# One masked square a head in the even linear attention, and outputs five steps behind scores in the softmax attentions

## The reference

```python
def step(s, blk):
    qc, kc, vc, gc = blk
    G = jnp.cumsum(gc, axis=2)
    decay = jnp.exp(jnp.where(tri, G[:, :, :, None, :] - G[:, :, None, :, :], -jnp.inf))
    scores = jnp.einsum('bhik,bhjk,bhijk->bhij', qc, kc, decay)
    o = jnp.einsum('bhij,bhjv->bhiv', scores, vc) + jnp.einsum('bhik,bhkv->bhiv', qc * jnp.exp(G), s)
    G_last = G[:, :, -1:, :]
    s = s * jnp.exp(G_last)[:, :, 0, :, None] + jnp.einsum('bhjk,bhjv->bhkv', kc * jnp.exp(G_last - G), vc)
    return s, o
```

## Time and profile before

| What | us |
|---|---|
| median of three runs | 3082.21 |
| the profiled execution, its own time | 3080.94 |
| its span in the profile | 3079.1 |
| TensorE busy | 2976.5 |
| VectorE busy | 732.1 |
| ScalarE busy | 399.4 |
| GpSimd busy | 252.1 |
| even layer's softmax attention | about 217 to 270 |
| GLA | 270 to 378 |
| attentions of the second stack | 1559 to 1595 and 2009 to 2050 |

### The profile page before, as it was taken

One profiled execution on the slowest core, in us unless ns is written; L12 is line 12 of the kernel. 1 busy time (PEld: TensorE's weight loads), 2 busy tenths in 40 slices (PEclk: granted clock), 3 DMA queues, 4 the chain that ended last, 5 costly groups with the idle time before them and its releaser, 6 DMA issues.

```text
span 3079.1 us, 41222 instructions
## 1 busy us (share of the span) xinstructions
PE 2976.5 (97%) x17952; PEld 1702.2 (55%) x17952; DVE 732.1 (24%) x1737; ACT 399.4 (13%) x981; POOL 252.1 (8%) x339
## 2 busy tenths in 40 slices
PE   7999899999999999999999999999999999999998
PEld 3546654444459998667657777454444444444434
DVE  1327722000046665400141001242000000000002
ACT  1114220000022222100031000131000000000001
POOL 2113310000012221200000000000000000000030
PEclk9999999999999999999999999999999999999999
DMA  9860022122122222354335332319999999999993
GB/s 361 320 256 3 15 82 82 60 84 82 57 72 59 76 76 84 117 191 157 122 111 205 143 143 103 127 55 392 361 402 385 385 402 384 384 403 385 384 404 122
DMA packets 214210, 618.59 MB, mean 201 GB/s; under 512 B 6840, under 2 KB 54168, under 8 KB 207504
## 3 DMA queue, kind: packets, MB, share of 16 engines
q1 hardware_dynamic: 206128, 594.30, 50.9%
q0 software_dynamic: 7296, 20.54, 2.0%
q10 hardware_dynamic: 608, 1.12, 0.1%
HBM read 608.67 MB, written 7.26 MB: 200 GB/s over the span
## 4 chain that ended last, share of the span: by engine, by line
PE 91%; DVE 3%; DMA 2%; issue 2%; ACT 1%; PEld 0%; PEldq 0%; POOLq 0%; POOL 0%; DVEq 0%; SPq 0%; ACTq 0%
PE ps_main L677 15%; PE ps_main L719 7%; PE ps_moe_down L3329 6%; PE ps_moe_up L3279 6%; PE ps_moe_gate L3279 6%; PE ps_second L677 6%; PE ps_main L2120 6%; PE ps_lin L1516 4%; PE ps_moe_down L3337 3%; PE ps_moe_gate L3284 3%; PE ps_moe_up L3284 3%; PE ps_second L719 3%; PE ps_main L2143 2%; PE ps_main L564 1%; PE ps_mod L1445 1%
## 5 line engine op out<-in xcount | busy, mean ns | idle before, releaser
L677 PE MATMUL ps_main<-hT,ring_buf 128*128 128x256 f32 (+2 forms) x1408 | 447.9, 479 | 2.4 <-issue 1.6
L677 PEld LDWEIGHTS ps_main<-hT,ring_buf 128*128 128x128 f32 x1408 | 263.7, 190 | 187.0 <-issue 169.2
L719 PE MATMUL ps_main<-ring_buf,ffn_hiddenT 128*128 128x512 f32 x528 | 228.9, 593 | 1.8 <-issue 1.8
L2120 PE MATMUL ps_main<-ring_buf,hT 128*128 128x256 f32 (+1 forms) x992 | 196.1, 352 | 0.3 <-issue 0.3
L677 PE MATMUL ps_second<-hT,ring_buf 128*128 128x256 f32 (+1 forms) x896 | 192.3, 376 | 2.3 <-DMA ring_buf<-in_w_ffn_up_dram 1.0
L3502 DVE TENSOR_TENSOR moe_hidden_buf<-moe_silu_buf,ps_moe_up 128x768 f32<-128x768 f32 (+1 forms) x32 | 27.3, 854 | 664.7 <-PE ps_moe_up L3284 664.7
L677 PEld LDWEIGHTS ps_second<-hT,ring_buf 128*128 128x128 f32 x896 | 167.1, 190 | 28.4 <-issue 5.3
L2120 PEld LDWEIGHTS ps_main<-ring_buf,hT 128*128 128x128 f32 x992 | 166.4, 191 | 17.8 <-issue 0.6
L719 PEld LDWEIGHTS ps_main<-ring_buf,ffn_hiddenT 128*128 128x128 f32 x528 | 99.5, 190 | 127.7 <-issue 127.6
L1516 PE MATMUL ps_lin<-ring_buf,hT 128*128 128x448 f32 (+1 forms) x384 | 133.1, 500 | 1.0 <-ACT hT L1576 1.0
L3279 PE MATMUL ps_moe_up<-ring_buf,moe_xg_buf 128*64 128x512 f32 (+1 forms) x672 | 131.8, 545 | 0.0
(11 more groups left out here) (547 smaller groups left out, 3524.3 us busy)
## 6 DMA issues: line engine op xcount, KB each, us to landing
ring_buf<-in_w_exp_down_dram SPq DMA_DIRECT2D x17, 4096.0 KB, 18.5
ring_buf<-in_w_exp_up_dram SPq DMA_DIRECT2D x16, 4096.0 KB, 18.7
ring_buf<-in_w_exp_gate_dram SPq DMA_DIRECT2D x15, 4096.0 KB, 19.8
mod_pieces<-in_mod_w_dram SPq DMA_DIRECT2D x40, 1024.0 KB, 6.5
moe_third<-in_w_exp_gate_dram SPq DMA_DIRECT2D x9, 4096.0 KB, 19.6
moe_third<-in_w_exp_up_dram SPq DMA_DIRECT2D x8, 4096.0 KB, 19.1
moe_third<-in_w_exp_down_dram SPq DMA_DIRECT2D x7, 4096.0 KB, 18.5
ring_buf<-in_odd_w_in_dram SPq DMA_DIRECT2D x40, 512.0 KB, 6.2
```

The lines of the kernel that those rows point to most:

```text
L677: mm = nc.tensor.matmul(ps[:, lo:wide], view[:, k, i * P:(i + 1) * P], hT[:, k, first_col + lo:first_col + wide], start=k == 0, stop=k == ...
L719: mm = nc.tensor.matmul(ps_y[i % 2][:, h, :], hidT[:, b, i * P:(i + 1) * P], view[:, b, h * 512:(h + 1) * 512], start=first, stop=end)
L2120: mm = nc.tensor.matmul(ps[:, 0:width], hT[:, k, t * P:(t + 1) * P], view[:, k, 0:width], start=k == 0, stop=k == KD - 1)
```

## The change

**In GLA** the two coarsest levels are handled apart. Their scores are made for the blocks alone that the mask would leave, one of 64 x 64 and two of 32 x 32 for each head (`coarse_blocks`), and ScalarE copies these into the square (`take_coarse`). VectorE then lays the other six levels over the same square, one predicated copy each, so that one square a head stays, cleared once at the start; the output has one product a head for it. The scores' banks are split in two: levels 0 to 3, and 4 to 6 with the own keys. TensorE may fill the first once two levels of the unit before have been merged. Sums of the six fine levels use half of the rows (a fine block never crosses the middle of the tile), with 384 columns. The end keys go from VectorE to GpSimd, behind the keys; the total is made by ScalarE. TensorE's list becomes scores(u), output(u-1), sums(u+3).

**In `attend`** there are three probability buffers in place of two. In step i TensorE runs scores(i), turned(i-3), output(i-5); VectorE takes the turned copy ahead of the division. The buffer of turned probabilities keeps two halves.

```diff
@@ gla_pairs @@
-        PLACES, ROUNDS = 2, NL // 2
+        ROUNDS, COARSE = NL - 2, 2
+        HALF, QUARTER = P // 2, P // 4
...
+            def coarse_blocks(d):
+                late, early = (0, 1) if d == 0 else (1, 0)
+                return [(0, late * HALF, early * HALF, HALF)] + \
+                    [(1, x * HALF + late * QUARTER, x * HALF + early * QUARTER, QUARTER) for x in range(2)]
...
                 def sums(u):
                     pe.wait_ge(S["rec_decays"].handle, S["rec_decays"].at(u))
-                    for h in range(2):
-                        nc.tensor.matmul(ps_sums[:, h * 4:h * 4 + 4, :], gs(u), T.sums[:, units[u][1], h * 4:h * 4 + 4, :],
+                    table = T.sums[:, units[u][1], :, :]
+                    for c in range(2):
+                        nc.tensor.matmul(ps_sums[:, c, 0:2, :], gs(u), table[:, 0:2, c * HALF:(c + 1) * HALF],
+                                         start=True, stop=True)
+                    for c in range(2):
+                        own = slice(c * HALF, (c + 1) * HALF)
+                        nc.tensor.matmul(ps_sums[:, c, 2:NL, :], gs(u)[own, :], table[own, 2:NL, own],
                                          start=True, stop=True)
...
-                    pe.wait_ge(S["rec_masked"].handle, S["rec_masked"].at(u))
-                    for l in range(NL - 1):
+                    pe.wait_ge(C["coarse_taken"].handle, C["coarse_taken"].at(u))
+                    pe.wait_ge(S["rec_masked"].handle, S["rec_masked"].at(max(ROUNDS * (u - 1) + 2, 0)))
+                    for l, k0, q0, size in coarse_blocks(d):
                         for e in range(2):
-                            nc.tensor.matmul(ps_scores[:, e, l, :], kd[lanes(e), u % 2, l, :], qd[lanes(e), u % 3, l + 1, :],
-                                             start=True, stop=True)
+                            nc.tensor.matmul(ps_scores[0][k0:k0 + size, e, l, q0:q0 + size],
+                                             kd[lanes(e), u % 2, l, k0:k0 + size], qd[lanes(e), u % 3, l + 1, q0:q0 + size],
+                                             start=True, stop=True, tile_position=(e * GK, k0))
+                    for l in range(COARSE, NL - 1):
+                        if l == 4:
+                            mm.then_inc(C["coarse_made"].handle, 1)
+                            pe.wait_ge(S["rec_masked"].handle, S["rec_masked"].at(ROUNDS * u))
...
                     for e in range(2):
-                        for s in range(PLACES):
-                            mm = nc.tensor.matmul(ps_out[:, e, :], merged[:, u % 2, e, s, :], vs(u, e),
...
+                        mm = nc.tensor.matmul(ps_out[:, e, :], merged[:, u % 2, e, :], vs(u, e),
+                                              start=fresh(u), stop=fresh(u) or e == 1)
...
                     scores(u)
+                    if u >= 1:
+                        output(u - 1)
                     if u + 3 < n:
                         sums(u + 3)
-                    if u >= 1:
-                        output(u - 1)
...
+                def take_coarse(u):
+                    d = units[u][1]
+                    act.wait_ge(C["coarse_made"].handle, C["coarse_made"].at(u + 1))
...
+                    for l, k0, q0, size in coarse_blocks(d):
+                        last = nc.scalar.activation(merged[k0:k0 + size, u % 2, :, q0:q0 + size],
+                                                    ps_scores[0][k0:k0 + size, :, l, q0:q0 + size], ACT.Copy)
...
+                    if u + 2 < n:
+                        decays(u + 2)
+                    take_coarse(u)
...
+                    nc.gpsimd.tensor_tensor(k_end[:, u % 3, :], ks(u), rest_decay[:, u % 2, :], ALU.mult)\
+                        .then_inc(C["ends_made"].handle, 1)
...
-                    nc.vector.tensor_copy(total[:, u % 4:u % 4 + 1], decay[:, u % 2, 0, end:end + 1])
-                    nc.vector.tensor_tensor(k_end[:, u % 3, :], ks(u), rest_decay[:, u % 2, :], ALU.mult)
...
                     for r in range(ROUNDS):
-                        levels = slice(r * PLACES, (r + 1) * PLACES)
...
+                        level = COARSE + r
+                        which = T.mask[:, d, level, :].unsqueeze(1).to_broadcast([P, 2, P])
+                        if level == 4:
+                            dve.wait_ge(S["rec_scores"].handle, S["rec_scores"].at(u + 1))
...
+                        nc.vector.copy_predicated(mine, which.bitcast(I32), ps_scores[level // 4][:, :, level % 4, :])\
+                            .then_inc(S["rec_masked"].handle, 1)
@@ attend @@
-            probs = sb(cx, "att_probs_buf", [P, 2, 2, nkt * P + own_column])
+            probs = sb(cx, "att_probs_buf", [P, 3, 2, nkt * P + own_column])
...
-                for i in range(n + 3):
+                for i in range(n + 5):
...
-                    if 2 <= i < n + 2:
-                        turned(i - 2)
-                    if i >= 3:
-                        output(i - 3)
+                    if 3 <= i < n + 3:
+                        turned(i - 3)
+                    if i >= 5:
+                        output(i - 5)
...
-                    act.wait_ge(S["att_turned"].handle, S["att_turned"].at(u - 1))
+                    act.wait_ge(S["att_turned"].handle, S["att_turned"].at(u - 2))
...
+                    if i >= 3:
+                        take_turned(i - 3)
                     if 1 <= i <= n:
                         shares(i - 1)
-                    if i >= 2:
-                        take_turned(i - 2)
```

More of the change, by code:

```diff
@@ L863, in gla_pairs @@
             kT = sb(cx, "pair_kT", [P, 2, 4, P])
-            total = sb(cx, "pair_total", [P, 4])
+            total = sb(cx, "pair_total", [P, 8])
             squares = sb(cx, "pair_square_sums", [P, 4, GH])
@@ L867, in gla_pairs @@
             junk = sb(cx, "pair_junk", [P, GV])
-            ps_scores = bank[:, 0:4, :].rearrange("p (e b) (l n) -> p e (b l) n", e=2, n=P)
-            ps_sums = bank[:, 4:6, :].rearrange("p b (l n) -> p (b l) n", n=P)
+            staged = bank[:, 0:4, :].rearrange("p (w b) (l n) -> p w (b l) n", w=2, n=P)
+            ps_scores = [bank[:, 2 * b:2 * b + 2, :].rearrange("p e (l n) -> p e l n", n=P) for b in range(2)]
+            ps_sums = bank[:, 4:6, :].rearrange("p c (l n) -> p c l n", n=HALF)
             bank_out, bank_rest = bank[:, 6, :], bank[:, 7, :]
@@ L953, in decays @@
                         act.wait_ge(S["rec_k"].handle, S["rec_k"].at(u - 1))
-                    nc.scalar.activation(decay[:, u % 2, :, :], ps_sums[:, :, :], ACT.Exp, scale=1.0 / 16.0)
+                        act.wait_ge(C["ends_made"].handle, C["ends_made"].at(u - 1))
+                    nc.scalar.activation(decay[:, u % 2, :, :].rearrange("p l (c n) -> p c l n", c=2), ps_sums, ACT.Exp,
+                                         scale=1.0 / 16.0)
+                    c, n = (1, HALF - 1) if units[u][1] == 0 else (0, 0)
+                    nc.scalar.activation(total[:, u % 8:u % 8 + 1], ps_sums[:, c, 0, n:n + 1], ACT.Exp, scale=1.0 / 16.0)
                     nc.scalar.activation(rest_decay[:, u % 2, :], ps_rest, ACT.Exp, scale=1.0 / 16.0)\
@@ L1062, in take @@
                         elif not final(u):
-                            last = nc.vector.scalar_tensor_tensor(out=own, in0=own, scalar=total[lanes(e), u % 4:u % 4 + 1],
+                            last = nc.vector.scalar_tensor_tensor(out=own, in0=own, scalar=total[lanes(e), u % 8:u % 8 + 1],
                                                                   in1=ps_state[lanes(e), :], op0=ALU.mult, op1=ALU.add)
@@ L1301, in _ @@
                     link_v(nc.vector.tensor_scalar(minus[:, :], sinks[:, 0:4 * kv_heads], -1.0, None, ALU.mult))
-                for i in range(n + 2):
+                for i in range(n + 3):
                     if i < n:
```

68 lines of the change are left out of this document (37 added, 31 removed).

## The result

The changed kernel takes 3098.07 us (median of four, 3095.85 to 3101.98) where the kernel before takes 3081.57; the ratio is 1.0057 with an interval of 1.0045 to 1.0070. The forecast was 3079.6, its range 3073.5 to 3086.0. It is slower by more than this kernel's measurement leaves open. Rival 3, the one on that side, had another reason: a dearer unit of the linear attention.

What follows compares the result with a forecast made beforehand. TensorE was taken to bound the kernel, busy in 97% of the span. GLA -5.6, even attention +3.0 and second attentions 0 made -2.6 us on 3080.94: 3078.3, as median 3079.6; range 3073.5 to 3086.

Steps and rivals of the forecast that it cites:

- Rival 3: GLA: small matmuls cost 0.11 us, borders 0.2; unit 6.7, whole 3091; chance 0.15 from 5.9 up, 0.05 from 6.4.
- the step that failed: Softmax attentions, while scores are left: the two-deep room for transposed probabilities costs nothing, since VectorE's work takes longer.
- The tail: Softmax attentions after the last scores: a serial chain, 12.4 us against 8.15 in the even one, about 2 more in others.
- a low clock in GLA: Sign against the forecast: the clock in the GLA stretch falling below the 1.00 seen before.
- 12c + 10.95: GLA, first to last merge, with c TensorE's time a unit: 79.4 us against 85.0, 5.6 won.
- c: TensorE's time for one GLA unit after the change: 5.7 us, bounds 5.0 to 6.1, against 5.82 before.
- the sign that the prediction named: GLA: the forecast is wrong if TensorE's unit is under 5.4 us or over 6.0.
- The borders: TensorE's GLA unit: eight changes of tile shape in place of three, 0.18 us each, 1.44 in all.
- rival 1: GLA: borders between tile shapes are cheap, unit up to 5.3 us; GLA -10, attentions +3, whole 3075; chance 0.22.
- The coarse scores: TensorE's GLA unit: twelve small instructions, between 0.36 and 1.3 us, taken as 0.5; 0.9 with their borders.
- The sums: TensorE's GLA unit: 1.33 us by plain prices where it was 1.94; about 1.7 with their borders.
- Rival 4: GLA: ScalarE's coarse copies behind late decays delay merges 0.5 us a unit; GLA +0, whole 3085; chance 0.07.

Runs made afterwards that it cites:

- the moved rest: The changed linear attention with the softmax attentions of before, the matmul for the rest of the tile moved beside the full-row sums: 3076.8 us, one run.
- the moved sums: The changed linear attention with the softmax attentions of before, TensorE's sums put ahead of the output: 3071.62 us, one run.
- full sums: The changed linear attention with the softmax attentions of before, sums of all eight levels over all rows again: 3072.94 us, one run.

## Why the prediction was wrong

On the profiled executions the forecast was 3078.3 and 3098.88 came. Of these 20.6 us the two attentions of the second stack make 13.8 (forecast 0), the even one 4.4 (7.4 for 3.0), and the stretches that the forecast left alone 7.5; the linear attention takes back 5.1.

**The attentions: the step that failed.** It reads: "While scores are left, they run under the copies and it costs nothing: VectorE's own work, and not this ring, is the longer way." I saw that the copy of unit u now waits for an output directly behind transposes u, but followed it only to TensorE. I left out what that output waits for: there is one output bank, so it waits for a take, and the take stands in ScalarE's list behind two exponentials, which stand behind the very copy. So the ring is closed on ScalarE while scores are left as well. Four units of the second stack, from one staging of keys to the next at full clock:

| Kernel | us |
|---|---|
| two buffers, outputs three on (before) | 7.74 |
| three buffers, outputs five on (the change) | 8.76 |
| the change, take ahead | 7.28 |
| the change, room for three turned units | 7.58 |
| three buffers, outputs four on | 7.57 |
| outputs four on, take ahead | 6.96 |

The two edits that open the ring at different places both take the loss away, and moving one output into the attention of before brings it. This is shown. In the first attention's body as a whole the loss is smaller than by this table (29.80 us against 28.56 at full clock), since the second key head is staged 1.4 us earlier with the change (8.2 us from the start for 9.6).

**The tail.** Its mechanism was right. In the even attention the last maxima start at 266.56 and end, read as in the forecast, at 267.70; the next stage starts at 281.29: 13.6 us for a forecast of 12.4 and 8.15 before. But the maxima come 1.9 us later after the attention's start, where I had them 1.3 earlier, for the ring is closed in the body. Both make the 7.4 us; forecast was 3.0. (Before, three units to be turned and four outputs stand behind the last scores; the list ahead of the prediction leaves out its last two rows, the last unit turned and two outputs.) In the second stack, from the start of the last scores to the next stage took 6.92 us before and 9.73 with the ring closed but without exponentials in it, at full clock: +2.8 for my 2. The change's own took 14.01.

**The clock, which the forecast had at nothing for the attentions.** Of the 10.0 us in the first attention of the second stack, 1.2 are the ring in the body (29.80 at full clock against 28.56) and 1.7 the lower clock there (31.48 against 29.80). For the tail, the window over the last one of the softmax attentions alone is nearly at full clock:

```profile
2067.54:2079.23 11.69, 6.62 (x58) 4.03 (x57) 4.74 (x21) 5.05 (x20) 0.00 (x0) 0.92 0.00 0
```

It took 11.69 us where the last attention of before has 7.20. By this estimate, taken over from the last attention to the first, about 4.5 of the tail's 7.1 come from the chain and some 2.6 from the clock; the granted clock is 0.70 and 0.57 in the two quarters from 1583 on. Another 1.9 us lie in the matmuls behind it, where the clock is 0.61 for the first 5 us. I wrote that a low clock in GLA would make the forecast wrong; it came in the attentions.

The other executions say how much that may be in all. Over a whole execution the changed kernel had a mean granted clock of 0.985 to 0.989; the kernel before had 0.991 to 0.995 in all but one of those with a clock on record. That one, at 0.988, took 3091.57 us, and the changed kernel at 0.988 took 3095.85 and 3097.27. So at the same mean clock the change loses about 5 us and not 16.5: an estimate, from few executions, that some 11 us of the net loss go with the clock, and that the rings cost the 10.7 that the linear attention won and about 5 more.

**The linear attention.** The sum 12c + 10.95 held: with the measured c = 5.35 it gives 75.2, and 75.2 was measured. That is not luck: its terms are each within some 0.3 us (the first step 4.18 for 4.5, the last two 5.01 and 3.87 for 4.95 and 3.85). What was mis-sized is c, forecast 5.7; the sign that the prediction named, a unit under 5.4, is there. The borders were not cheap, as rival 1 had it: beside the coarse group the unit stands 1.1 us over its plain prices, and taking one border away saves 0.20 us at the same instructions, close to the 0.18 forecast. The coarse scores were: 0.46 us with their borders where I had 0.5 without and 0.9 with them. The sums went the other way, 1.91 for 1.7. By the Trainium skill (TensorEngine Tiling (Array Packing), Key Properties), a change of tiling mode drains the engine; the moved rest and the moved sums agree with it, at 0.20 us each. VectorE's unit was 5.01 (forecast 4.95), GpSimd's end keys 0.46 (0.5), both as forecast. Rival 4's wait, for the coarse copies, is there: 0.6 us in every second unit of the middle, where TensorE sets the pace anyway.

The sum with the right terms, from the two traces: +7.4 - 10.7 + 10.0 + 1.9 + 3.8 + 1.6 + 4.0 = 18.0, of which 4.0 is ahead of all that was changed.

**What stays open.** Why the clock falls in one attention and not in the other. It was 1.00 from the first merge to the last in all fourteen kernels profiled. In the three that close the ring with the exponentials in it (the change, its softmax attentions alone, the attention of before with outputs a step later) it fell in both attentions of the second stack. But it did so too in the attentions of before beside the moved rest (a quarter at 0.76 in the one, at 0.69 in the other), and with the ring open it fell in the last (43.28 us, above). The attention of before, the same code, took 40.98 and 41.12 us in its last place with a low start, and 36.90 without one. So how much of the change's loss is clock will differ from run to run, and that closing the ring brings the low clock is not shown.

## What to carry to other kernels

Before an output is moved later in a software pipeline, compare its distance behind the producer with the depth of every buffer between them, and follow each wait around through the in-order lists of all engines until it ends at work already done: here a room two deep allows a distance of one. Where an instruction that frees a single bank stands behind long ones in a list, try it ahead of them; it won 0.15 and 0.37 us a unit here, and nothing in the attention of before. And count borders between tile shapes as well as columns: putting like shapes side by side brought 0.2 us each, as much as halving the rows of the sums.

## What the runs showed of the hardware

- The granted clock of TensorE was down to 0.50 in a quarter of an attention, the 1.2 GHz level, and back at 1.00 (2.4 GHz) later. Of the fourteen kernels profiled, twelve had a low stretch in one of the second stack's two attentions or right behind one; outputs four steps on and full sums had not. The same attention took 40.98 and 41.12 us with a low start and 36.90 without.
- Twelve matmul instructions on 64*64 and 32*32 tiles took 0.46 us, borders included; at the 0.056 us of a 64-row one they would have been 0.67 without.
- One change of tile shape fewer in a unit of the linear attention saved 0.20 us, in two different places (the sums from 1.91 to 1.71 us, the unit from 5.35 to 5.15).
- The stretch up to the even attention, the same code in all kernels, took between 217.4 and 221.9 us.
